# Two transformer blocks on one core: another order of work in the attention loop, and output products of a fourth block begun inside it

## What is computed

```python
def dsa_mixer(h, w_in, kv_norm_g, w_uk, w_uv, w_o, rel_bias):
    q, c, qi, ki, wi = jnp.split(h @ w_in, ATT_IN_SPLITS, axis=-1)
    ...
    q_lat = jnp.einsum('bshd,hdc->bshc', q, w_uk) * ATT_SCALE
    ...
        logits = jnp.einsum('bqhc,bqkc->bqhk', q_lat_b, c_sel).astype(jnp.float32) \
            + bias.astype(jnp.float32)
        logits = jnp.where((dist >= 0)[:, :, None, :], logits, -jnp.inf)
        p = jax.nn.softmax(logits, axis=-1).astype(c.dtype)
    ...
    return o @ w_o
```

## Time and profile before

| | us |
|---|---|
| time, median of 3 runs | 848.88 |
| lowest and highest of them | 848.77, 849.24 |
| the profiled execution: time | 848.88 |
| the profiled execution: span | 847.1 |
| PE busy in the span | 841.7 |
| DVE busy | 651.4 |
| ACT busy | 509.5 |
| attention loop (logits of pair 0 to the wait for the last `oh`) | 311.7 to 354.1 |
| closing chain of the layer | 354.1 to 372.0 |

### The profile page before, as it was taken

One profiled execution on the slowest core, in us unless ns is written; L12 is line 12 of the kernel. 1 busy time (PEld: TensorE's weight loads), 2 busy tenths in 40 slices (PEclk: granted clock), 3 DMA queues, 4 the chain that ended last, 5 costly groups with the idle time before them and its releaser, 6 DMA issues.

```text
span 847.1 us, 17483 instructions
## 1 busy us (share of the span) xinstructions
PE 841.7 (99%) x7152; PEld 817.9 (97%) x7152; DVE 651.4 (77%) x1237; ACT 509.5 (60%) x925; POOL 43.8 (5%) x63
## 2 busy tenths in 40 slices
PE   9999999999999999999999999999999999999998
PEld 7999999999999997899999999999999999999998
DVE  6978668898977689786668555566699889998873
ACT  5795777774435568678778444434447685445650
POOL 0000000000000126100000000021020000000000
PEclk9999999999999999999999999999999999999999
DMA  9927868878987824287657856516554424456541
GB/s 302 347 68 223 278 213 262 274 260 282 300 264 231 282 69 140 61 257 237 207 177 214 243 190 200 195 55 167 162 195 150 150 77 142 156 172 193 168 142 51
DMA packets 162866, 164.23 MB, mean 194 GB/s; under 512 B 16817, under 2 KB 159329, under 8 KB 162529
## 3 DMA queue, kind: packets, MB, share of 16 engines
q1 hardware_dynamic: 161696, 162.05, 60.2%
q10 hardware_dynamic: 1088, 1.05, 0.4%
HBM read 162.01 MB, written 2.91 MB: 195 GB/s over the span
## 4 chain that ended last, share of the span: by engine, by line
PE 96%; DVE 2%; DMA 1%; ACT 0%; POOL 0%; issue 0%; ACTq 0%; DVEq 0%
PE ps L316 25%; PE ps L320 25%; PE ps L318 25%; PE ps L442 3%; PE ps L1612 2%; PE ps L1614 2%; PE ps L1610 2%; PE ps L459 2%; PE ps L1703 1%; PE ps L1707 1%; PE ps L1705 1%; PE ps L1672 1%; PE ps L1661 1%; PE ps L1652 1%; PE ps L1138 1%; PE ps L1158 1%
## 5 line engine op out<-in xcount | busy, mean ns | idle before, releaser
L283 DVE TENSOR_TENSOR wl<-raw,wh 128x1024 fp32r<-128x1024 f32 x256 | 310.5, 1229 | 27.0 <-ACT wh L276 26.7
L316 PE MATMUL ps<-xh,wh 128*128 128x256 f32 x1136 | 319.4, 281 | 0.0
L320 PE MATMUL ps<-xh,wl 128*128 128x256 f32 x1136 | 315.5, 278 | 0.1
L318 PE MATMUL ps<-xl,wh 128*128 128x256 f32 x1136 | 315.4, 278 | 0.0
L276 ACT ACTIVATE wh<-raw 128x1024 fp32r<-128x1024 f32 x256 | 267.4, 1053 | 73.8 <-PE ps L320 66.3
L316 PEld LDWEIGHTS ps<-xh,wh 128*128 128x128 f32 x1136 | 213.6, 188 | 4.8 <-issue 2.8
L318 PEld LDWEIGHTS ps<-xl,wh 128*128 128x128 f32 x1136 | 213.8, 188 | 0.4 <-DVE xl L384 0.2
L320 PEld LDWEIGHTS ps<-xh,wl 128*128 128x128 f32 x1136 | 213.8, 188 | 0.4 <-DVE wl L283 0.3
L320 PE MATMUL ps<-hh,wl 128*128 128x256 f32 x512 | 141.3, 276 | 0.0
L316 PE MATMUL ps<-hh,wh 128*128 128x256 f32 x512 | 141.3, 276 | 0.0
L318 PE MATMUL ps<-hl,wh 128*128 128x256 f32 x512 | 141.3, 276 | 0.0
(11 more groups left out here) (363 smaller groups left out, 1378.5 us busy)
## 6 DMA issues: line engine op xcount, KB each, us to landing
raw<-in_w_in_dram SPq DMA_DIRECT2D x34, 1024.0 KB, 5.2
raw<-in_mlp_up_dram SPq DMA_DIRECT2D x32, 1024.0 KB, 5.5
raw<-in_mlp_down_dram SPq DMA_DIRECT2D x32, 1024.0 KB, 6.6
aw<-in_w_adaT_dram SPq DMA_DIRECT2D x24, 512.0 KB, 4.6
raw<-in_rec_w_in_dram SPq DMA_DIRECT2D x7, 1024.0 KB, 11.6
raw<-in_att_w_in_dram SPq DMA_DIRECT2D x6, 1024.0 KB, 5.5
raw<-in_rec_w_out_dram SPq DMA_DIRECT2D x4, 1024.0 KB, 6.0
raw<-in_att_w_o_dram SPq DMA_DIRECT2D x4, 1024.0 KB, 5.5
```

The lines of the kernel that those rows point to most:

```text
L283: e.tensor_tensor(parts_of(i)[1], raw_of(i), f32(parts_of(i)[0]), op=ALU.subtract).then_inc(S["wl"], 1)
L316: e.matmul(o, H[:, first + n], xh[:, k], start=start and n == 0, stop=False)
L318: e.matmul(o, H[:, first + n], xl[:, k], start=False, stop=False)
L320: ins = e.matmul(o, L[:, first + n], xh[:, k], start=False, stop=stop and n == len(ks) - 1)
```

## The change

Three things are moved; no instruction is added or removed.

```diff
-    QSTEPS = (0, 0, 0, 1, 2, 3, 4, 5)
+    QSTEPS = (0, 0, 1, 2, 3, 4, 5, 6)
 
-    WO_BESIDE = {6: ((0, 0, 3),), 7: ((0, 3, 4), (1, 0, 4)), 8: ((2, 0, 5),),
-                 9: ((0, 4, 6), (1, 4, 6), (2, 5, 6)), 10: ((0, 6, 7), (1, 6, 7), (2, 6, 7))}
+    WO_BESIDE = {7: ((0, 0, 4),), 8: ((1, 0, 5),), 9: ((2, 0, 6), (0, 4, 6)),
+                 10: ((3, 0, 6), (1, 5, 7), (0, 6, 7), (2, 6, 7), (3, 6, 7))}
...
-        for f in range(3):
+        for f in range(4):
             tensor_wo(e, q, f, 7, 8)
-        for f in range(3, 8):
+        for f in range(4, 8):
             tensor_wo(e, q, f, 0, 8)
...
         for k in range(11):
+            if k > 2:
+                vector_divided(e, q, k - 3)
+            if 2 <= k < 10:
+                vector_ratios(e, q, k - 2)
             if k < 8:
                 vector_logits(e, q, 2 * k)
+                if k == 0:
+                    vector_q(e, q, 1)
+                vector_logits(e, q, 2 * k + 1)
+            if k > 2:
+                vector_outputs(e, q, k - 3)
             if k == 0:
-                vector_q(e, q, 1)
-            if k > 2:
-                vector_divided(e, q, k - 3)
-            if k < 8:
-                vector_logits(e, q, 2 * k + 1)
-            if 2 <= k < 10:
-                vector_ratios(e, q, k - 2)
-            if k == 0:
-                lows(e, q, at["q5"] + 1)
                 vector_q(e, q, 2)
                 vector_q(e, q, 3)
-            if k > 2:
-                vector_outputs(e, q, k - 3)
...
             if k > 2:
                 scalar_ratios(e, q, k - 3)
+                scalar_outputs(e, q, k - 3)
             if k < 8:
                 scalar_exp(e, q, 2 * k)
-            if k > 2:
-                scalar_outputs(e, q, k - 3)
-            if k < 8:
                 scalar_exp(e, q, 2 * k + 1)
```

## The result

The changed kernel took 853.77 us (median of 8 runs, 850.84 to 855.72) against 849.17 us for the kernel before on the same chip (8 runs, 848.77 to 849.7). The ratio is 1.0051, 95% interval 1.0036 to 1.0066. The direction was right. The time is 0.8 us outside the range of 849.8 to 853.0.

What follows compares the result with a forecast made beforehand. It took PE as the bound, 841.7 of 847.1 us busy, and added loop waits of 1.5 and 0.2, a closing-chain loss of 0.9 and 0.1 for a square to 848.88: 851.6 us, range 849.8 to 853.0.

Steps and rivals of the forecast that it cites:

- the last one: Final sum: 2.6 us of loop waits and closing-chain loss, 0.1 for a square, on 848.88, giving 851.6 us.
- q5's split in pass 0: Start of the loop: the low split of q5's weight stands behind q4's scaling on DVE; PE waits 0.5 us.
- The ring: Loop between ACT and DVE: `divided`, logits and exponentials wait in a circle, 4.1 us a pass, 5.0 with a `wh`.
- The scaling of q7: Moved to the end of pass 6 on DVE; PE's pair-7 logits wait about 1.5 us for it, 1.0 to 2.0.
- the term of `outputs`: Pass 6 on DVE, ahead of q7's scaling: `outputs` meets POOL's add in flight and takes 0.83 us.
- Values of pair 5: They reuse the bank of head 14's logits; PE waits 0 to 0.5 us, taken as 0.2.
- The closing chain: End of layer: DVE's rigid 16.07 us starts later behind the longer filler; PE waits 1.8 us for `xl`, loss 0.9.
- What the layer cost: Loop waits of 1.5 and 0.2 us plus 0.9 for the closing chain: 2.6 us, and 0.1 for the square.
- Rival (b): Closing chain follows PE, with DVE's chain under 14.3 us: 848.0 us, not slower; chance 0.07.
- Rival (a): Only the closing chain costs, q7 is scaled before PE wants it: 849.8 to 850.2 us; chance 0.20.

Runs made afterwards that it cites:

- r1: The changed kernel again, unaltered, in another set of runs: 851.89 us, ratio 1.0037 to the kernel before.
- r3: Kernel before with its old order on DVE and ACT, but the new `QSTEPS`, `WO_BESIDE` and tile ranges (filler of 33): 849.73 us, ratio 1.0012.
- r4: Kernel before with only the new order on DVE and ACT, old tables and q5's split early as before: 850.05 us, ratio 1.0016.
- r5: Changed kernel with q7 scaled ahead of `outputs` of its pass: 852.92 us, ratio 1.0054.
- r2: Changed kernel with its new order, but 12 filler matmuls in pass 10 instead of 33: 849.08 us, ratio 1.0000.
- r7: Kernel before with its old order on DVE and ACT, but the new `QSTEPS` and 12 filler matmuls in pass 10: 847.07 us, ratio 0.9989.
- r10: r7 with the first x add of the closing chain waiting for wo2 instead of wo0: 848.00 us, ratio 0.9995.
- r11: r7 with the first x add of the closing chain waiting for wo3 instead of wo0: 852.11 us, ratio 1.0037.
- r6: Changed kernel with the low split of wo5's weight made ahead of the closing chain's first x add: 852.07 us, ratio 1.0040.
- r8: r7 with 15 filler matmuls in pass 10 and wo5's weight split made ahead of the closing chain: 848.26 us, ratio 0.9999.
- r9: r3 with 27 filler matmuls in pass 10 instead of 33: 849.31 us, ratio 1.0008.

## Why the prediction was wrong

**The step that failed is the last one**, "848.88 + 2.7 = 851.6 us": a sum of engine times at a clock that was taken to stay as it was. PE's wait of 1.8 us at the end of the chain was forecast, but priced at 1.8 us. In about half of the executions (5 of the 8 timed ones here, 3 of 6 in r1) it costs about 1.8 us more, since the granted clock goes to 1.2 GHz for 3.4 us behind it. That put the median of 853.77 us 1.7 us above the 852.06 of the runs at full clock, and 0.8 us outside the range. That these runs came so close to 851.6 is partly luck: they lie 2.9 us above before, the same kernel in r1 only 1.8. The Trainium skill ("TensorE: Matmul & The Clock Gate", "The HAM clock gate") says that the clock has two levels and that PE's activity decides between them. The traces agree, with 1.00 and 0.50 and windows between them only at the edges, and a PE that was busy for 0.99 of 2.0 us before the fall. I should have made it a rival: a forecast wait of PE in a layer that had none of that length before.

**q5's split in pass 0**: right. Wait 0.4 us, forecast 0.5.

**The ring**: right in kind, a little too large. The `divided` starts are 323.98, 328.87, 332.88, 338.10 and 342.12, so passes with a `wh` took 4.9 and 5.2 us (forecast 5.0), the others 4.0 (4.1). r3 shows that without the new order none of it is there, and r4 that the order alone makes it. The forecast let DVE's own work delay the third `divided` (4.4 us behind the second); it took 4.01, and the fourth one came at 338.10, 0.5 us earlier than forecast when this execution's start, 0.49 us ahead, is taken off.

**The scaling of q7**: the term of `outputs` was mis-sized. I gave it 0.83 us because it would meet an add of POOL. It took 0.33 up to the next start. POOL's add of a head is two instructions, and `outputs` (339.97) came just ahead of the second (339.99): the add was held up, not DVE. The Trainium skill ("SBUF — State Buffer", "SBUF: two separate sides", on the exclusive lock of the shared pair) says that whoever starts first keeps it for the whole instruction. The trace agrees, both here and the other way round in r5, where `outputs` came later and took 0.70. I had used the rule with the wrong one in front. PE's wait was 0.81 instead of 1.5 us: 0.5 less by `outputs`, 0.5 less by the earlier `divided`, and 0.3 more since PE was there 0.15 us sooner than forecast and its logits began 0.15 us behind the end of the scaling, not 0.04. The 0.49 us of the early start play no part, as they move both engines.

**Values of pair 5**: 0.42 us, forecast 0.2, inside its bounds of 0 to 0.5. Together the loop's waits are 1.2 us instead of 1.7.

**The closing chain**: right. 16.06 us (16.07), first x add at 357.31, which is 357.8 less the 0.5 us of the loop (forecast 356.6 + 1.7 = 358.3, less the 0.49 at the start). PE stood 1.82 us up to that `xl` (1.8). Without the long filler the stand is gone (r2, r7), and r10 and r11 show that the start of DVE's chain does it and nothing on PE. The forecast loss of 0.9 us against before had q5's 0.5 in it; the 0.4 left is 0.1 in r3 up to the last `xl` and 0.3 up to the norm. One thing was wrong in it: the chain is not DVE's work alone. r6 took a split of 1.13 us out and it got 0.2 shorter, since a step can't be shorter than ACT's `xh` lets it. Rival (b), a chain that yields, is out. Rival (a) is out too, as q7 was late in every profile with the new order and the new tables.

**What the layer cost**: 2.15 us up to the last `xl`, forecast 2.6 (and 0.1 for the square behind it). The 0.5 us between them are the loop's.

**Still open**: the two runs at 0.996. They fit two stretches at the lower level, but none of them was profiled, so where the second lies isn't shown. The wait for q7 is the likely place: PE was busy for only 3.77 of the 5 us from 340 to 345, as little as for the 3.78 from 369 to 374. That is argued, not measured, and r2, with the same waits there and 11 runs at 1.000, speaks against it being enough by itself.

## What to carry to other kernels

A filler that covers a wait of PE also delays everything that hangs on the tile behind it. Before lengthening it, look for an engine whose chain starts there, and add up that chain: with 14 of 15 us busy it can't catch up. r7 stops at 12 matmuls instead of 33, leaves a short wait at the last `oh`, and wins 0.11 to 0.14%. The same goes for work put into an engine's idle time ahead of a chain: in r8 the split was longer than the gap and delayed the chain by 1.1 us. And price a new wait of the matrix engine not only by its length. Where several follow each other with little work between, look at the granted clock of every run and not only of the profiled one.

## What the runs showed of the hardware that was not expected

The lower clock doesn't need a long stand: here no single bracket before a fall was over 0.70 us, and the clock fell 1.0 (r11) to 1.5 us (r6) after PE had gone back to full work, not during the waits. Whether it falls differs between executions of one kernel with equal waits (5 of 12 in r3).

At full granted clock, matmuls of one kind (128x256, each with its own weights) run at one of two paces, 0.113 or 0.118 us from start to start, for tens of microseconds, and an execution changes between them mostly where small matmuls interrupt the row. In r1, the same kernel as after, the pace is the longer one from 374.8 to 380.4 and the shorter one from there to 416, the reverse of after. So the changed kernel doesn't force it. Whether it makes it likelier is open: of the fourteen profiles, six have 172 or 173 matmuls from 380 to 400 us (after, r5, r6, r8, r10, r11) and eight have 179, and all six are of kernels whose PE was late at the chain's end, as are three of the eight (r1, r3, r9). One profile of a kernel can't show more. The pace can move an execution by 1.4 us, as the account of after shows. Times at full clock scatter by more than that: 847.67 to 850.42 for before, beside r1, and 847.41 to 851.33 for r9. So two kernels that differ by 1 us need ten runs each or more, and the account of one profiled execution should end with how many matmuls each window holds. What sets the pace was not tried.
